# Four weight buffers of a matmul-bound kernel, begun at four different offsets in SBUF

## The reference, cut to what matters

```
# block 1, for each of two layers
h = rms_norm(x, norm_g)
proj = h @ w_in                      # q, k, v, z of attention, conv, retention, gates
a = diff_attention(...) * silu(az);  c = short_conv(...) * silu(cz);  r = retention(...) * silu(rz)
merged = sum_i sigmoid(gates_i) * (branches_i @ w_branch[i])
x = x + merged @ w_out
# block 2, for each of two layers
h = rms_norm(x, norm_g_2)
proj = h @ w_in_2                    # conv, latents of q and kv, gates, spatial gating
y = [conv branch, latent attention (w_uq, w_ukv), spatial gating branch], each normed and gated
x = x + y @ w_out_2
```

## Time and profile before

| | |
|---|---|
| median of 3 runs | 3651.8 us (3651.55 to 3652.79) |
| the profiled execution | 3651.65 us, its span 3649.8 us |
| granted TensorE clock, mean | 0.994 of 2.4 GHz |
| PE busy | 98% of the span, 16568 matmuls |
| PE weight load busy | 76% |
| DVE, POOL, ACT busy | 50%, 38%, 30% |

### The profile page before, as it was taken

The page is one execution under the profiler, slowest core; times in us unless marked ns, Lnnn a source line. Parts: engine busy times, 40 slices in busy tenths (PEclk is TensorE's granted clock), DMA queues, the critical chain, the costliest instruction groups (busy, mean ns, idle before and its releaser), DMA issues.

```text
span 3649.8 us, 42601 instructions
## 1 busy us (share of the span) xinstructions
PE 3582.0 (98%) x16568; PEld 2787.2 (76%) x16568; DVE 1832.9 (50%) x2191; ACT 1085.6 (30%) x1811; POOL 1393.5 (38%) x670
## 2 busy tenths in 40 slices
PE   8999999999999999999999999999999999999999
PEld 6777888888878767788888878777766678776667
DVE  5764032233156675113233236884766579566663
ACT  3443111102212335100102213223565331445542
POOL 2222343432356222344442347443432255342324
PEclk9999999999999999999999999999999999999999
DMA  4110111111134101111111124311110231111122
GB/s 163 30 35 26 58 49 47 49 49 35 38 109 141 31 29 30 48 55 49 43 53 40 35 58 133 105 47 30 52 29 27 80 127 49 39 47 35 31 68 93
DMA packets 69644, 209.23 MB, mean 57 GB/s; under 512 B 7536, under 2 KB 8560, under 8 KB 68976
## 3 DMA queue, kind: packets, MB, share of 16 engines
q1 hardware_dynamic: 48960, 159.08, 14.7%
q10 hardware_dynamic: 20528, 47.91, 3.7%
HBM read 185.99 MB, written 20.97 MB: 57 GB/s over the span
## 4 chain that ended last, share of the span: by engine, by line
PE 91%; DVE 5%; ACT 2%; issue 1%; DMA 0%; POOL 0%; SPq 0%; ACTq 0%; DVEq 0%; POOLq 0%
PE psA L501 47%; PE psT L482 17%; PE psA L482 8%; PE psA L1865 3%; PE psT L1936 2%; PE psT L783 2%; PE psA L735 2%; PE psT L1847 1%; PE psT L719 1%; PE psT L1913 1%; PE psT L1842 1%; DVE b_wk L2392 1%; PE psT L501 1%; PE psT L1910 1%; DVE b_wk L1318 0%
## 5 line engine op out<-in xcount | busy, mean ns | idle before, releaser
L448 POOL TENSOR_TENSOR Whi<-stage,credit 128x1024 fp32r<-128x1024 f32 (+1 forms) x332 | 597.3, 1799 | 2210.1 <-PE psA L501 1107.9
L451 POOL TENSOR_TENSOR Wlo<-stage,Whi 128x1024 fp32r<-128x1024 f32 (+1 forms) x332 | 795.8, 2397 | 26.0
L501 PE MATMUL psA<-Hhi,Whi 128*128 128x512 f32 x2208 | 689.7, 394 | 0.4 <-DVE b_ypad L2382 0.4
L501 PE MATMUL psA<-Hlo,Whi 128*128 128x512 f32 x2208 | 680.2, 389 | 0.0
L501 PE MATMUL psA<-Hhi,Wlo 128*128 128x512 f32 x2208 | 679.8, 389 | 0.0
L501 PEld LDWEIGHTS psA<-Hhi,Whi 128*128 128x128 f32 x2208 | 413.3, 188 | 95.7 <-issue 12.1
L501 PEld LDWEIGHTS psA<-Hhi,Wlo 128*128 128x128 f32 x2208 | 414.4, 188 | 86.6
L501 PEld LDWEIGHTS psA<-Hlo,Whi 128*128 128x128 f32 x2208 | 414.4, 188 | 86.6
L482 PE MATMUL psT<-Hhi,Whi 128*128 128x512 f32 x1024 | 417.8, 408 | 8.2 <-POOL Wlo L451 3.1
L482 PE MATMUL psT<-Hhi,Wlo 128*128 128x512 f32 x1024 | 402.7, 393 | 0.0
L482 PE MATMUL psT<-Hlo,Whi 128*128 128x512 f32 x1024 | 401.8, 392 | 0.0
(11 more groups left out here) (327 smaller groups left out, 4885.1 us busy)
## 6 DMA issues: line engine op xcount, KB each, us to landing
stage<-in_w SPq DMA_DIRECT2D x264, 512.0 KB, 3.5
stage<-in_w SPq DMA_DIRECT2D x68, 256.0 KB, 2.6
xs<-X ACTq DMA_DIRECT2D x8, 2048.0 KB, 8.4
b_wk<-xs ACTq DMA_DIRECT2D x32, 256.0 KB, 3.9
b_wk<-xs ACTq DMA_DIRECT2D x14, 512.0 KB, 4.2
rope<-in_ropes ACTq DMA_DIRECT2D x4, 1024.0 KB, 4.8
out<-b_wk ACTq DMA_DIRECT2D x8, 512.0 KB, 2.6
b_wk<-in_x ACTq DMA_DIRECT2D x4, 512.0 KB, 10.3
```

Of the source, the lines that this page charges most:

```text
L448: pool.tensor_tensor(Whi[:, b, 0:n], stage[:, b, 0:n], credit[:, 0:1].broadcast_to([P, n]), ALU.add).then_inc(s.w_hi, 1)
L451: pool.tensor_tensor(Wlo[:, b, 0:n], stage[:, b, 0:n], Whi[:, b, 0:n].bitcast(F32), ALU.subtract).then_inc(s.w_split, 1)
L501: mm = pe.matmul(dst[h], w[:, cols], r[k][:, h * HALF:(h + 1) * HALF], start=first and k == order[0] and r is rhi and w is whi, stop=last ...
```

## The change

```diff
+        ident = sb("ident", [P, P])
+        ones = sb("ones", [P, P])
+        identb = sb("identb", [P, P], BF16)
+        maskb = sb("maskb", [P, P], BF16)
+        sb("pad_x", [P, 384])
         X = sb("X", [P, KT, SEQ])
         Hhi = sb("Hhi", [P, KT, SEQ], F32R)
         Hlo = sb("Hlo", [P, KT, SEQ], F32R)
         stage = sb("stage", [P, 2, KT * P])
-        Whi = sb("Whi", [P, 2, KT * P], F32R)
-        Wlo = sb("Wlo", [P, 2, KT * P], F32R)
-        ident = sb("ident", [P, P])
-        ones = sb("ones", [P, P])
-        identb = sb("identb", [P, P], BF16)
-        maskb = sb("maskb", [P, P], BF16)
+        sb("pad_whi0", [P, 16])
+        Whi0 = sb("Whi0", [P, KT * P], F32R)
+        sb("pad_whi1", [P, 48])
+        Whi1 = sb("Whi1", [P, KT * P], F32R)
+        sb("pad_wlo0", [P, 64])
+        Wlo0 = sb("Wlo0", [P, KT * P], F32R)
+        sb("pad_wlo1", [P, 96])
+        Wlo1 = sb("Wlo1", [P, KT * P], F32R)
+        Whi, Wlo = (Whi0, Whi1), (Wlo0, Wlo1)
+        sb("pad_rope", [P, 160])
         rope = sb("rope", [P, 2, SEQ])
...
-                                pool.tensor_tensor(Whi[:, b, 0:n], stage[:, b, 0:n],
+                                pool.tensor_tensor(Whi[b][:, 0:n], stage[:, b, 0:n],
...
-                three_pass(pe, psA[:, A.buf(name)], env.Whi[:, p % 2], env.Wlo[:, p % 2],
+                three_pass(pe, psA[:, A.buf(name)], env.Whi[p % 2][:], env.Wlo[p % 2][:],
...
-    nc = bacc.Bacc("TRN2", target_bir_lowering=False, num_devices=1, dynamic_dma_scratch_size=4096)
+    nc = bacc.Bacc("TRN2", target_bir_lowering=False, num_devices=1, dynamic_dma_scratch_size=1024)
```

More of the change, by code:

```diff
@@ L446, in _ @@
                                 pool.wait_ge(s.panel_begun, L * NP + p0 + b + 1 + base + i * 2)
-                                pool.tensor_tensor(Whi[:, b, 0:n], stage[:, b, 0:n],
+                                pool.tensor_tensor(Whi[b][:, 0:n], stage[:, b, 0:n],
                                                    credit[:, 0:1].broadcast_to([P, n]), ALU.add).then_inc(s.w_hi, 1)
                                 pool.wait_ge(s.w_hi, L * NP + p0 + b + 1 + base + i * 2)
-                                pool.tensor_tensor(Wlo[:, b, 0:n], stage[:, b, 0:n], Whi[:, b, 0:n].bitcast(F32),
+                                pool.tensor_tensor(Wlo[b][:, 0:n], stage[:, b, 0:n], Whi[b][:, 0:n].bitcast(F32),
                                                    ALU.subtract).then_inc(s.w_split, 1)
@@ L702, in half_panel @@
                     pe.wait_ge(*A.room(L, name))
-                mm = three_pass_half(pe, psA[:, A.buf(name), cols(half)], env.Whi[:, p % 2], env.Wlo[:, p % 2],
+                mm = three_pass_half(pe, psA[:, A.buf(name), cols(half)], env.Whi[p % 2][:], env.Wlo[p % 2][:],
                                      [Hhi[:, k] for k in range(KT)], [Hlo[:, k] for k in range(KT)], KT, P, half,
@@ L763, in piece @@
                 if kind in ("q", "k", "v", "z") or kind in EARLY:
-                    mm = three_pass_half(pe, psF, env.Whi[:, p % 2], env.Wlo[:, p % 2],
+                    mm = three_pass_half(pe, psF, env.Whi[p % 2][:], env.Wlo[p % 2][:],
                                          [Hhi[:, k] for k in range(KT)], [Hlo[:, k] for k in range(KT)], KT, P,
@@ L973, in tensor @@
                         pe.wait_ge(*A.drained(L, ("branch", 2, KT - 2 + n)))
-                    three_pass_half(pe, OUT[n % 2], env.Whi[:, p % 2], env.Wlo[:, p % 2],
+                    three_pass_half(pe, OUT[n % 2], env.Whi[p % 2][:], env.Wlo[p % 2][:],
                                     [Hhi[:, k] for k in range(KT)], [Hlo[:, k] for k in range(KT)], KT, P, half,
@@ L1832, in panel @@
                 tiles = tiles or range(nk)
-                mm = three_pass(pe, dst, env.Whi[:, p % 2], env.Wlo[:, p % 2], [Hhi[:, k] for k in tiles],
+                mm = three_pass(pe, dst, env.Whi[p % 2][:], env.Wlo[p % 2][:], [Hhi[:, k] for k in tiles],
                                 [Hlo[:, k] for k in tiles], nk, M, s.panel_begun, first, last,
@@ L1895, in piece @@
                     nk, t0 = (Q_LORA_T, 0) if kind == "q" else (KV_LORA_T, Q_LORA_T)
-                    mm = three_pass_half(pe, psF, env.Whi[:, w % 2, t0 * P:], env.Wlo[:, w % 2, t0 * P:],
+                    mm = three_pass_half(pe, psF, env.Whi[w % 2][:, t0 * P:], env.Wlo[w % 2][:, t0 * P:],
                                          [Hhi[:, t0 + k] for k in range(nk)], [Hlo[:, t0 + k] for k in range(nk)],
@@ L1901, in piece @@
                 elif kind == "o":
-                    mm = three_pass_half(pe, psF, env.Whi[:, w % 2], env.Wlo[:, w % 2], [Hhi[:, k] for k in O_TILES],
+                    mm = three_pass_half(pe, psF, env.Whi[w % 2][:], env.Wlo[w % 2][:], [Hhi[:, k] for k in O_TILES],
                                          [Hlo[:, k] for k in O_TILES], len(O_TILES), P, half,
@@ L1982, in opening @@
                         pe.wait_ge(*x_ready.upto(1 + L, (15 + b if L == 0 else 13 + b + 2 * half) if half == 0 or L else 16))
-                        mm = three_pass_half(pe, psA[:, b, cols(half)], env.Whi[:, p % 2], env.Wlo[:, p % 2],
+                        mm = three_pass_half(pe, psA[:, b, cols(half)], env.Whi[p % 2][:], env.Wlo[p % 2][:],
                                              [Hhi[:, k] for k in range(KT)], [Hlo[:, k] for k in range(KT)], KT, P,
@@ L2078, in tensor @@
                         pe.wait_ge(*x_ready.upto(2 + L, n - 3))
-                    three_pass_half(pe, OUT_BANKS[n % 4], env.Whi[:, w % 2, part], env.Wlo[:, w % 2, part],
+                    three_pass_half(pe, OUT_BANKS[n % 4], env.Whi[w % 2][:, part], env.Wlo[w % 2][:, part],
                                     [Hhi[:, 2 + k] for k in range(4)], [Hlo[:, 2 + k] for k in range(4)], 4, P, half,
```

## The result

| | before | changed |
|---|---|---|
| median | 3651.7 us (3649.3 to 3652.8, 4 runs) | 3704.4 us (3702.4 to 3708.0, 4 runs) |
| ratio, 95% interval | 1 | 1.0145 (1.0132 to 1.0157) |
| profiled execution: time, span | 3651.65, 3649.8 us | 3702.44, 3700.3 us |

A forecast was written before the change was run, and what follows sets the result against it. TensorE, busy 98% of the span, was taken as the bound: 12384 matmuls at 226.7 ns, 2807 us. Every term was 0, so 3651.65 us + 0, forecast as the median 3651.8 us, range 3580 to 3705.

The forecast's parts named there:

- Which buffers: Matmuls by weight buffer: Whi0 4384 at 64, Whi1 3872 at 256, Wlo1 1936 at 384, Wlo0 2192 unchanged; 10192 get another distance.
- Three things speak for no: Matmuls with weights at another distance: claimed their pace stays 226.7 ns, on three arguments; 0 us.
- The first argument: Matmul stream: bank collisions would let DVE and POOL spread the distance, but 226.7 ns is the same in every stretch; 0 ns.
- The second: Weights against activations in a panel: all relations mod 1024, 2048 and 4096 have one pace, only 512 or less is untested; 0 ns.
- The third, the sweep: Weight load and moving reader: one sweeps past the other through every relation mod 512, so the start hardly matters; 0 ns.
- The bounds: Matmul stream: from below all of the 10.8 ns gone, -110 us; from above a second helping of the 13.4 ns, +137 us.
- Rival B: Matmul stream slower: distance 0 is the good phase, others meet more often; 5 ns more in 10192 matmuls, +51 us, 3703; chance 0.13.
- Rival A: Matmul stream faster: at distance 0 both reads hinder each other, any other start ends it; in full 110 us, 3541 us; chance 0.23.
- The 2.6 ns of float32: Float32 matmuls of 512 columns: 429.2 ns, two times 213.3 and 2.6 more, so 10.8 of the 13.4 are peculiar to float32r.
- the distance in the long piece: Longest piece in the chain of waits: keeps 226.7 ns if the forecast is right; another distance makes it wrong.
- Panels of even and odd number would show two distances: Sign in the panels for Rival A or Rival B: the pace must differ by buffer; no size given.
- Wlo0's matmuls would stand at 226.7 beside others that moved: Sign in the panels for Rival A or Rival B: Wlo0, at its old distance, keeps 226.7 ns.

The follow-up runs named there:

- e7: Stream of matmuls alone, blocks of 48: distances in 4-byte steps, mixed distances, 384 and 256 columns, float32; 512 columns float32r took 226.7 ns at 0, 233.3 at 64.
- e3: Changed kernel with paddings that put all four weight buffers at distance 256 bytes from the moving tiles; 3652.7 us, ratio 0.9998 to the kernel before.
- e5: Changed kernel with only Whi0 left at distance 64, the three other weight buffers at 0; 3681.6 us, ratio 1.0078 to the kernel before.
- e6: Changed kernel with only Wlo1 left at distance 384 (128 by the period), the other weight buffers at 0; 3674.3 us, ratio 1.0059 to the kernel before.
- e1: Changed kernel with all four weight buffers back at distance 0 from the moving tiles, other parts of the change kept; 3652.8 us, ratio 0.9998 to the kernel before.
- e4: Stream of matmuls alone, 48 for each distance of 0 to 496 bytes in steps of 16, then moving tiles 64 later; nothing under 226.7 ns.
- e10: Stream of matmuls alone: distances 0, 16, -16, 64, 192, each in 11 blocks behind a matmul of another length; 226.7 ns in all at 0, 233.3 at 64.

## Why the prediction was wrong

**What bounds the kernel:** right. The count of 12384, 226.7 ns each and the question of whether that hangs on the weights' place were the whole matter. The 213.3 ns for 512 columns are what e7 gives (0.417 ns a column), and the 13.4 beside them (13.3 by e7) are the same for 256, 384 and 512 columns at distance 0; whether they are the weight load's stays open.

**Which buffers:** 10192 matmuls at another distance was wrong. By the period of 256 Whi1 kept its place (e3, 226.7 ns at 256), and the matmuls of all four buffers changed pace: one displaced buffer raised its whole panels, to 232.3 ns in e5 and 232.2 in e6.

**"Do they get another pace? Three things speak for no":** this is the step that failed, and it failed by its value of 0 ns. The measured value is 5.6 ns in the long pieces, 232.3 for 226.7, because the pace hangs on the distance modulo 256 bytes (e1 to e4).
- The first argument (DVE and POOL don't spread the distance) is true, also in the changed kernel (432 matmuls in 100 us with DVE busy for 7.33 and for 39.93), and says nothing here. What changed is between the matmuls and the weight loads, and these keep step: from 450 to 700 us of both traces every weight load starts 2 to 4 ns behind the matmul ahead of it.
- The second (all relations mod 1024, 2048 and 4096 have one pace, only 512 or less is untested) was true, and I let an untested case count as a tested one. All of the 12384 matmuls stood at a single distance modulo 256.
- The third, the sweep, was wrong as an argument. That a load takes at most 0.111 us, and passes through every relation once, was my estimate from the earlier trace rows; no run shows at which moment a load or a matmul reads its bytes. And I took one pass through every relation to mean that the start doesn't count. e7 shows that 4 bytes of start do (226.7 at 0, 233.3 at -4, 232.4 at +4), and e10 that, at -16 and 192, what stands ahead of a block decides its steady pace (226.7 or 228.3, 228.9 or 233.3 ns). That the first matmuls of a block are off their steady pace could be seen before: the earlier trace rows is the approach to 226.7, in starts 231, 236, 228, 232, 231, 227. I had read it as a matter of its own that I couldn't tie to addresses.

**The bounds:** from +137 us to -110 us they held it. Rival B had the direction, and its condition that 0 is the good distance is what the sweep shows for 512 columns. Its cause, "the load reads the lines that the moving reader has just left", isn't shown by any run. I gave it 0.13. That its 3703 us stand beside 3704.4 is in part luck: it took 5 ns, from the slow starts of the earlier trace rows, for 10192 matmuls, where the runs have 5.4 ns in long stretches and 4.0 in short groups, and all 12384 pay. The range ended at 3705 because that rival's sum stood there. Rival A had the sign wrong: no distance tried is better than 0 at 512 columns, and the 10.8 ns over the float32 stream were nothing that a distance gives back. The 2.6 ns of float32, and the half pace beside float32r, are those of one record of 429.2 ns; a float32 matmul of 512 columns leaves two of them (e7: 41.20 us for 48 matmuls, 858 ns each), so neither is a number of a whole matmul.

**The sum, afterwards,** worked out from the starts in the two traces. Stretches of more than 60 of these matmuls on end make 8280 of the 12384; their mean distance, without those of 300 ns and more, went from 226.8 to 232.2 ns, +44 us. The other 4104 stand in short groups between other work, where before the first distances of a group already cost (228.0 ns); they went to 232.0, +17 us. That would be 61 us. With the long distances in (the first matmul of a group, pauses, the clock at 0.50) all distances between them add up to 53.9 us more, and the rest of the kernel takes 2.4 us less; the two spans differ by 50.5. A part of the 7 us between 61 and 54 is the clock. In the stretches of 3.4 and 6.8 us at a granted clock of 0.50 these matmuls start 427 ns apart, 1.2 columns a ns; that cost them about 9 us before and about 5 now. The other 3 us aren't split further. Between the medians the change is 52.7 us. The rows are those of spans and granted clock, before and after:

```profile
core 0: 3649.8 us, clock 0.994
```
```profile
core 0: 3700.3 us, clock 0.997
```

**The signs that I named:** the distance in the long piece decided, as written. "Panels of even and odd number would show two distances" was no good sign: both mixtures happen to have 232.3. "Wlo0's matmuls would stand at 226.7 beside others that moved" was wrong as well: in e5 the loads of Wlo0, at distance 0 among displaced ones of Whi0, are at 232.2.

**Float32r and float32.** In this float32r stream the place of the weights changes the pace by 6.7 ns of 226.7 between the distances 0 and 64 (e4); for float32 it changes nothing at 0, 64 and 128 (429.2 ns a record, e7).

No version beat the kernel before. e1 and e3 equal it, and all the others are slower.

## What to carry to other kernels

In a stream of float32r matmuls of 512 columns that each load fresh weights, let the weight tiles and the moving tiles begin at the same place modulo 256 bytes, exactly (4 bytes, the smallest step tried, were enough to lose it); by these runs another distance mostly costs 1 to 3% of such a stream (192: 228.9, 64: 233.3, 96: 234.2 against 226.7 ns). With 384 columns 0 was the best of three distances, with 256 it was the worst of them. It is worth a look at allocations, since a small tensor or a padding ahead of the weights sets it by accident, and one misplaced buffer slows the matmuls of its neighbour too (e6: odd panels at 232.2 ns for 226.9, with one load in three displaced). For the reader of profiles: when one number is the same in every row, ask whether the rows differ in the thing that is about to change; here they did not, and a sweep of 48 matmuls for each distance, in one kernel of 655 us, would have told.

## What the runs showed of the hardware that was not expected

- The pace of float32r matmuls of 512 columns with fresh weights changes with the distance of the operands in a partition: 226.7 ns at 0, 233.3 at 64, 234.2 at 96, and the sixteen distances from 256 to 496 bytes repeat those from 0 to 240 to 0.1 ns (e4).
- One displaced buffer raised the mean of its neighbour too: with only Wlo1 at 128 odd panels stand at 232.2 ns for 226.9, and the distances in which loads of Whi1 run, at distance 0, at 231.5 (e6).
- One distance can have two steady paces, by the matmul ahead of the block: 226.7 in six blocks and 228.3 to 228.4 in five at -16, 228.9 in ten and 233.3 in one at 192 (e10).
- For short moving operands 0 isn't always the best: 256 columns take 120.0 ns at 0, 117.8 at 64 and 118.7 at 128, while 384 take 173.3, 174.7 and 176.0 (e7).
- Float32 of 512 columns takes 429.2 ns a record, of which each matmul leaves two in the trace, at 0, 64 and 128 alike (e7).
- No run shows what the 13.3 ns over 213.3 at distance 0 go to, nor the 6.7 more at 64.
